# Third unit's query of layer 1 for the third chunk alone, first groups inside the attention; the latents' input projections of layer 0 half a unit later

## The reference, cut to what matters

```
q = (t @ w_query).reshape(nt, 8, 2, 128)
s1, s2 = q[:, :, 0] . sub_k1, q[:, :, 1] . sub_k2      # 128 scores each
v1, i1 = top_k(s1, 16); v2, i2 = top_k(s2, 16)
top_s, top_pos = top_k(v1[:, None] + v2[None, :], 16)  # 16 of 256 pairs
expert_idx = i1 * 128 + i2 at top_pos; gates = softmax(top_s)
out = sum_k gates_k * gelu(t . u_tab[expert_k]) * v_tab[expert_k]
```

## Time and profile before

| | us |
|---|---|
| median of 3 runs (2343.33 to 2344.27) | 2344.12 |
| the profiled execution | 2341.56 |
| its span | 2339.8 |
| busy: PE / DVE / ACT / POOL | 1639.4 / 1551.2 / 875.4 / 944.3 |
| moved by DMA | 927.92 MB, mean 397 GB/s |

### The profile page before, as it was taken

The page is one execution under the profiler, slowest core; times in us unless marked ns, Lnnn a source line. Parts: engine busy times, 40 slices in busy tenths (PEclk is TensorE's granted clock), DMA queues, the critical chain, the costliest instruction groups (busy, mean ns, idle before and its releaser), DMA issues.

```text
span 2339.8 us, 27431 instructions
## 1 busy us (share of the span) xinstructions
PE 1639.4 (70%) x9193; PEld 716.9 (31%) x9193; DVE 1551.2 (66%) x3640; ACT 875.4 (37%) x2596; POOL 944.3 (40%) x840
## 2 busy tenths in 40 slices
PE   7998987777876666766555766678787765555556
PEld 3655543323333222323211212225453311111111
DVE  1227767887767677777767676653868877766654
ACT  2223443445443233443333444442523333332323
POOL 1213244545453444444444454430343545444441
PEclk8999998889898878888777987888998877766788
DMA  9999899999999999999999999994699999999996
GB/s 398 384 370 354 343 390 420 421 420 416 420 413 420 420 419 414 415 414 417 413 417 411 421 420 419 417 388 162 266 386 418 419 422 421 421 421 421 422 421 290
DMA packets 140490, 927.92 MB, mean 397 GB/s; under 512 B 17063, under 2 KB 24007, under 8 KB 33342
## 3 DMA queue, kind: packets, MB, share of 16 engines
q0 software_dynamic: 112816, 807.16, 83.8%
q1 hardware_dynamic: 27390, 119.01, 12.8%
q10 hardware_dynamic: 144, 0.01, 0.0%
HBM read 924.97 MB, written 1.15 MB: 396 GB/s over the span
## 4 chain that ended last, share of the span: by engine, by line
DMA 45%; PE 27%; DVE 16%; issue 5%; ACT 5%; POOL 2%; SPq 0%; POOLq 0%; DVEq 0%; ACTq 0%
DMA arena<-in_uv,small 43%; PE bank L1465 13%; DVE arena L2412 8%; PE bank L797 3%; POOL arena L736 2%; PE bank L762 2%; ACT aux L1728 2%; DMA arena<-in_ada 1%; PE bank L153 1%; PE bank L783 1%; DVE aux L2334 1%; PE bank L944 1%; ACT small L1721 1%; PE bank L1278 1%; PE bank L774 1%
## 5 line engine op out<-in xcount | busy, mean ns | idle before, releaser
L736 POOL DMA_INDIRECT arena<-in_uv,small x765 | 898.9, 1175 | 1173.1 <-PE bank L1465 887.5
L1465 PE MATMUL bank<-arena,aux 64*64 64x512 f32 x5896 | 917.8, 768 | 620.7 <-ACT aux L1728 583.6
L2412 DVE CUSTOM_DVE_ANT_0 arena<-arena,h 128x1024 f32<-128x1024 f32 x765 | 922.8, 1228 | 460.5 <-DMA arena<-in_uv,small 454.2
L1465 PEld LDWEIGHTS bank<-arena,aux 64*64 64x64 f32 x5896 | 259.3, 171 | 1214.2 <-ACT aux L1728 695.7
L1721 ACT ACTIVATE small<-small 128x4 f32<-128x4 f32 (+3 forms) x212 | 43.4, 205 | 1097.0 <-DVE small L2412 1096.9
L1728 ACT ACTIVATE aux<-aux,small 128x64 f32<-128x64 f32 x768 | 206.4, 337 | 7.0 <-ACT small L1721 0.2
L1703 ACT ACTIVATE aux<-small 128x64 f32<-128x64 f32 x768 | 204.4, 336 | 11.6 <-DVEq L2403 2.6
L797 PE MATMUL bank<-hT,aux 128*128 128x256 f32 (+1 forms) x752 | 159.6, 367 | 4.7 <-ACT hT L1534 2.5
L797 PEld LDWEIGHTS bank<-hT,aux 128*128 128x128 f32 x752 | 130.2, 190 | 47.8 <-issue 27.0
L1675 ACT ACT_TABLE_LOAD x73 | 93.7, 1283 | 1.3
L2412 DVE DVE_READ_ACCUMULATOR2_ANT small<- 128x1 f32 x768 | 62.9, 82 | 0.0
(11 more groups left out here) (318 smaller groups left out, 1647.1 us busy)
## 6 DMA issues: line engine op xcount, KB each, us to landing
arena<-in_ada SPq DMA_DIRECT2D x36, 1024.0 KB, 10.3
aux<-in_w_query SPq DMA_DIRECT2D x43, 512.0 KB, 8.2
arena<-in_uv,small POOLq DMA_INDIRECT x765, 15.0
arena<-in_w_head SPq DMA_DIRECT2D x16, 512.0 KB, 10.1
hT<-in_ada SPq DMA_DIRECT2D x7, 1024.0 KB, 8.5
arena<-in_w_qkv SPq DMA_DIRECT2D x3, 2048.0 KB, 14.9
h<-in_ada SPq DMA_DIRECT2D x5, 1024.0 KB, 12.6
arena<-in_w_o SPq DMA_DIRECT2D x4, 1024.0 KB, 10.0
```

Of the source, the lines that this page charges most:

```text
L736: nc.gpsimd.indirect_dma_start(out=slot_at(pos), out_offset=None, in_=d["uv"][unit // FIRST], in_offset=bass.IndirectOffsetOnAxis(ap=self. ...
L1465: last = nc.tensor.matmul(bank[2 * r + m][out:out + 64, :], self.dg[rr, (s + o) % 8, :], slot_at(at)[rr, cols], start=first, stop=False)
L2412: last = nc.vector.tensor_tensor_reduce(out=slot_at(at)[:, 0:D], in0=slot_at(at)[:, 0:D], in1=h[:, c * D:(c + 1) * D], scale=1.0, scalar=0 ...
```

## The change

In layer 0 the input projections of the latents and the steps after them move four positions later, half a unit, up to the first head of the attention, whose last steps are squeezed into the old places:

```diff
 # PE, lat()
-                    yield 5
+                    yield 9
                     pe.wait_ge(nt_copied, 24)
                     in_half(2, 0, bank[6])
-                    yield 7
+                    yield 11
                     in_half(2, 1, bank[7])
 ...
-                    yield 10
+                    yield 15
                     in_half(3, 0, bank[6])
-                    yield 11
+                    yield 16
                     in_half(3, 1, bank[7])
 ...
-                    yield 21      # q_of(0), k_of(0)
+                    yield 25
-                    yield 29      # transposes_of(0)
+                    yield 30
 # ACT, lat()
-                    for c, at in ((2, 7), (3, 13)):
+                    for c, at in ((2, 11), (3, 17)):
 # DVE, lat()
-                    for c, at in ((2, 8), (3, 14)):      # an_mean, an_rope
+                    for c, at in ((2, 12), (3, 18)):
-                    yield 23
+                    yield 25
                     rotate_lat(0)
 # the ring: places 7 to 9 from slot 42, 11 until slot 37
-            early = [*range(7 if n < 34 else 10)]
-            return early + [11] * (n < 30) + [IN_ROWS] * (n >= 16)
+            early = [*range(7 if n < 42 else 10)]
+            return early + [11] * (n < 38) + [IN_ROWS] * (n >= 16)
```

In layer 1 the query of unit 34 is split. Chunk 2's half is made in `second_layer`, in bank 6, with its own copy, score and choice; chunk 3's half stays in `third_job`. Three groups of unit 32 instead of two lie inside the attention, and the first group of unit 33 comes before chunk 3's residual:

```diff
 # ring of layer 1
-        start = (9, 6, 0, 1, 10, 11, 7, 8) * 2 + (9, 6, 0, 1, 2, 3, 4, 5, 12, 13, 14)
+        start = (9, 6, 0, 1, 10, 11, 7, 8) * 3 + (2, 3, 4, 5, 12, 13, 14)
 # PE
+                def third_query():
+                    for side in range(2):
+                        pe.wait_ge(w_q_loaded[side], 32 + 48 * side)
+                        last = queries(self.wq_third[side], side, CTX, P, 0, bank[6])
+                    last.then_inc(q_done, 1)
+                def third_score():
+                    pe.wait_ge(o_copied, last_count(2 * H, 2 * H - 1))
+                    pe.wait_ge(third_stage, 1)
+                    score(0, self.keys_third).then_inc(third_stage, 1)
-                    g_attention(H, {0: next_score, 2: lambda: turned_transposes(7), 4: first_group, 5: tops_taken, 7: second_group})
-                    late_out(0, 3, 5)
-                    combine(FIRST, 2)
-                    late_out(0, 5, H)
-                    late_out(1)
-                    combine(FIRST, 3)
+                    g_attention(H, {0: next_score, 2: lambda: turned_transposes(7), 3: lambda: g_values(H + 1), 4: first_group,
+                                    5: lambda: combine(FIRST, 1), 7: lambda: combine(FIRST, 2), 8: lambda: late_out(0, 0, 3)})
+                    third_query()
+                    late_out(0, 3, 5)
+                    combine(FIRST, 3)
+                    third_score()
+                    late_out(0, 5, H)
+                    late_out(1)
+                    combine(FIRST + 1, 0)
 # ACT
-                    g_attention(H, {2: lambda: turned_copies(7), 3: first_group, 5: lambda: gates(FIRST + 1, False), 6: lambda: group(FIRST, 1)})
-                    group(FIRST, 2)
+                    g_attention(H, {2: first_group, 4: lambda: group(FIRST, 1), 6: third_group})
                     group(FIRST, 3)
+                    third_query_copy()
+                    gated_identities(FIRST + 1, 0)
+                    group(FIRST + 1, 0)
 # DVE
-                    g_attention(H, {0: lambda: raw_scale(7), 1: half_turned, 2: next_tops, 3: lambda: dots(FIRST, 0, range(GRP)),
-                                    4: lambda: choose(FIRST + 1, 1), 5: lambda: dots(FIRST, 1, (0, 1)), 6: lambda: dots(FIRST, 1, (2, 3))},
-                                {4: rest_chosen})
-                    dots(FIRST, 2, range(GRP))
+                    g_attention(H, {0: lambda: raw_scale(7), 1: half_turned, 2: lambda: dots(FIRST, 0, range(GRP)), 3: next_tops,
+                                    4: lambda: dots(FIRST, 1, range(GRP)), 5: lambda: choose(FIRST + 1, 1),
+                                    6: lambda: dots(FIRST, 2, range(GRP))},
+                                {5: rest_chosen})
                     dots(FIRST, 3, range(GRP))
                     finish_gates(FIRST + 1)
+                    dve.wait_ge(third_stage, 2)
+                    for side in range(2):
+                        tops_now(FIRST + 2, side, 0)
+                    dve.sem_inc(tops_done, 1)
+                    for stage in (1, 2, 3):
+                        choose(FIRST + 2, stage)
+                    dots(FIRST + 1, 0, range(GRP))
                     add_half(3, 0, bank[LATE_S[0]], self.ffn_rows1[0], gy_done, 2 * GKV + 1)
```

More of the change, by code:

```diff
@@ L402, in start_of, with ahead @@
             return n % FIRST == 0
+        def ahead(n, g):
+            return n == 0 and g < 2 or (n, g) == (FIRST + 1, 0)
         def idx_count(unit, half=1):
@@ L792, in k_proj, with queries @@
                     last.then_inc(kp_done, 1)
-                def queries(weights, side, lo, width, at):
+                def queries(weights, side, lo, width, at, b=Q_BANK):
                     for k in range(KD):
-                        last = nc.tensor.matmul(Q_BANK[:, side * 256 + at:side * 256 + at + width], weights[:, k, :], hT_at(k, lo, width),
+                        last = nc.tensor.matmul(b[:, side * 256 + at:side * 256 + at + width], weights[:, k, :], hT_at(k, lo, width),
                                                 start=(k == 0), stop=(k == KD - 1))
@@ L828, in third_job @@
                     for side in range(2):
-                        pe.wait_ge(w_q_loaded[side], 32 + 48 * side)
-                        queries(self.wq_third[side], side, CTX, 256, 0).then_inc(q_done, 1)
+                        last = queries(self.wq_third[side], side, CTX + P, P, P)
+                    last.then_inc(q_done, 1)
                 def third_scores():
                     pe.wait_ge(q_copied, 21)
-                    pe.wait_ge(tops_done, 18)
-                    score(0, self.keys_third)
+                    pe.wait_ge(tops_done, 19)
                     score(1, self.keys_third).then_inc(sc_done, 1)
@@ L1320, in g_attention @@
                             g_transposes(first + u - 1)
-                        if 2 <= u < H + 2:
+                        if 2 <= u < H + 2 and u != 3:
                             g_values(first + u - 2)
@@ L1482, in _ @@
                     for g in range(NG):
-                        if n or g > 1:
+                        if not ahead(n, g):
                             combine(n, g)
@@ L1648, in _, with third_query_copy @@
                 scored = S_BANK[:].rearrange("p (s c n) -> p s c n", s=2, c=2)
+                def third_query_copy():
+                    act.wait_ge(q_done, 35)
+                    act.wait_ge(sc_done, 18)
+                    nc.scalar.copy(self.qT[:, :, 0:P], bank[6][:].rearrange("p (s n) -> p s n", s=2)[:, :, 0:P]).then_inc(third_stage, 1)
                 def third_queries():
@@ L1783, in lat @@
                                 nc.scalar.copy(dst, src).then_inc(at_copied, 1)
-                    for c, at in ((2, 18), (3, 20)):
+                    for c, at in ((2, 22), (3, 24)):
                         yield at
@@ L2049, in g_attention @@
                             g_copies(first + u - 1)
-                        if u >= 2:
+                        if u >= 2 and u != 3:
                             g_out_copies(first + u - 2)
@@ L2771, in _ @@
                         elif n == FIRST + 1:
-                            if g == 1:
-                                dve.wait_ge(later_copied, 3)
-                                for side in range(2):
-                                    tops_now(n + 1, side, 0)
-                                dve.sem_inc(tops_done, 1)
-                                for stage in (1, 2, 3):
-                                    choose(n + 1, stage)
                             if g == 3:
```

40 lines of the change are left out of this document (20 added, 20 removed).

## The result

| | before | changed |
|---|---|---|
| median of 12 runs each, us | 2343.56 (2340.28 to 2345.09) | 2349.20 (2345.65 to 2355.61) |
| profiled execution / its span, us | 2341.56 / 2339.8 | 2345.77 / 2344.0 |
| first gather of layer 1, us | 1646.33 | 1642.37 |
| from there to the end of the span, us | 693.5 | 701.6 |

The ratio is 1.0027, interval [1.002, 1.0035]: slower, by 5.6 us between the medians, where 8 us faster were forecast. The last row tells where: layer 1 takes 8.1 us longer, and the 4.0 us by which it starts earlier cover half of that in this execution. In the changed kernel `combine` has line 1479, the gathers 739, the queries 800, the scores 808, `late_out` 1343, the ends of the norm 2231, the tops 2358.

What follows compares the result with a forecast made beforehand. The bound was taken to be one stream of 768 gathers of 1 MB, losing time only where its queue runs dry. Profiled 2341.6 - 8 (layer 0) + 0 (change of layers) = 2333.6; as median 2344.1 - 8 = 2336 us, range 2327 to 2346.

Steps and rivals of the forecast that it cites:

- part 2: Change of layers: 1.7 us gained at the gathers, 1.7 lost behind them; 0 in all, ends -6 and +6.
- part 1: Layer 0: chunk 2's `in_half` matmuls leave unit 0 and unit 1's first group; 8 us saved (3 to 11).
- what stands behind in part 2: Units 33 and 34 shift by 8 us behind the late third chunk; 1 to 3 us may go, 1.7 in the sum.
- the step that removes the hole: Layer 0 entry: `an_mean(2)` no longer stops DVE at 254.5, first gather issued at 259.4, not 272.1; the 5 us gap goes.
- slot 33's gather is issued at 289.3: Layer 0, unit 1: 2.3 us too late for the queue, landing at 294.7, not 304.6; stream 9.9 us ahead.
- 2 us for both, with 0 and 7 as ends: Layer 0: amount given back by the nine-place ring at slot 40 and DVE's wait for `rotate_lat(0)` at position 25.
- = 13.6 us: Change of layers, 1671 to slot 31: gathers 16, 20, 24, 28, 30 late by 1.8, 5.9, 2.2, 2.8, 0.9; before 15.3.
- they take it, the last by a hair: Units 33 and 34: slacks of 12.4 us at gather 39 and 8.3 at gather 55 absorb a shift of 8 us.
- the late third chunk decides: Rival, 0.12: unit 35's query chain 20 us late instead of 8, beyond 8.3 us of slack; 4 us slower, 2348.
- The rule weighed against a third group inside the attention: ACT, change of layers: skill page counts 2.66 us per table switch, 5.3 for the new pair; the row gave 2.6.

Runs made afterwards that it cites:

- e6: Kernel before with the second half of the third chunk's output projection computed twice, 7 us more on TensorE; 2349.34 us, ratio 1.0032.
- e3: Layer 1 part with only unit 32's three groups inside the attention and the new ring order, no split query, layer 0 as before; 2348.68 us, ratio 1.0036.
- e17: e3 with the third group of unit 32 taken out of the attention again; 2341.14 us, ratio 1.0007.
- e19: Changed kernel with the third group of unit 32 taken out of the attention again; 2343.73 us, ratio 1.0005.
- e7: Kernel before with the split query alone, groups, ring and latents unchanged; 2348.34 us, ratio 1.0027.
- e9: e7 with the late queries and score moved ahead of unit 33's second group on TensorE and ScalarE; 2339.55 us, ratio 0.9992.
- e18: e9 plus the change's layer 0 part, two groups of unit 32 inside the attention and the new ring; 2340.41 us, ratio 0.9996.
- e12: Kernel before with only the late queries and scores moved ahead of unit 33's second group on TensorE and ScalarE; 2339.34 us, ratio 0.9997.

## Why the prediction was wrong

Between 8 us faster and 5.6 us slower lie 13.6 us. 6.1 of them are the sum of the late gathers in part 2, 5.3 are part 1, 1.7 are what stands behind in part 2; 0.5 have no place.

**Part 1, the step that removes the hole: right.** No DVE wait before `an_mean` until 284 us, 420 GB/s from 260 to 280.

**Part 1, "slot 33's gather is issued at 289.3": 4.0 us off, and too much kept.** It was issued at 293.31. The wait of DVE was 8.06 us, as said; but PE, idle for 5.03 us, then started `combine(1, 2)` 1.5 us later than said and needed 6.5 us for it, not 3.66. Of what is given back, "2 us for both, with 0 and 7 as ends": the stream was 5.0 us ahead from 310 to 380 and 1.0 at 440, so about 4 went, in unit 3. The 4.0 us by which layer 1 starts earlier are not all gain either. Over twelve profiled executions with the old layer 0 the first gather of layer 1 lies between 1642.97 and 1648.70, mean 1646.5; over eight with the new one between 1642.37 and 1646.41, mean 1643.7. The part is worth about 2.7 us, not 8.

**Part 2, the sum "= 13.6 us" of the late gathers: the step that failed.** It was to be 1.7 us less than before and was 4.4 more: 19.1 against 14.7 in the stretches. The order of the chain and what each gather waits for were right, and gathers 8 and 12 did come earlier; the terms on PE were too small. In old times (3.96 us added) gathers 8, 12, 16, 20 and 24 were issued at 1668.7, 1679.8, 1694.4, 1710.9 and 1722.6, against 1667.1, 1676.9, 1690.5, 1706.4 and 1718.6 as forecast, and the norm was done at 1735.6 against 1731.3. Two terms come to these 4 us by their rows, though no run takes them apart. The combines of groups 1 and 2 stop PE and then take 5.36 us, priced at 3.66: 2 x 1.70 = 3.4 us, and `combine(32, 3)` and `late_out(1)` started 3.6 and 3.4 us later than said. And the forecast let the first gather go 1.9 us after the start of a `combine`; it went 2.8 us after it at groups 0 and 3. The other 2 of the 6.1 us stay open. Both terms stood in the trace of the kernel before, where the gathers after these rows were issued at 1673.66 and 1688.54:

```profile
1669.28 5.36 PE L1465 MATMUL bank<-arena,aux 64*64 64x512 f32 x32 [2.46 <-ACT aux L1728]
...
1685.75 3.66 PE L1465 MATMUL bank<-arena,aux 64*64 64x512 f32 x32
```

That this lateness costs in full is what e6 shows: 6.9 us lost for 6.9 us of delay, nearly all by gather 30, because gathers 20 to 31 wait in turn for `late_out(1)`, the norm and the third query with the queue dry. And without the third group inside most of the loss goes: 7.5 us of layer 1 from e3 to e17, 5.1 from the changed kernel to e19.

**Part 2, "they take it, the last by a hair": did not hold, for the same reason.** The forecast had unit 35 8 us late and 12.4 and 8.3 us of slack at gathers 39 and 55. Unit 35 was 11.6 us late. That is 3.3 us beyond the 8.3, and 3.4 us were lost, where the sum had 1.7. They were lost at gather 51, though, whose slack had not been read, so that the agreement may be luck.

**The rival that came nearest** was "the late third chunk decides" (chance 0.12, 2348 us). Its place was right: `combine(33, 2)` behind unit 35's query (e7 against e9). Its condition, a delay of 20 us that decides only from 16, was not: 11.6 us did, and most of the loss stood ahead of that `combine`. That its 2348 us lies near the measured 2349.2 is luck. Slower had a chance of 0.13 in all, too small for a sum whose two parts rested on the same price of a `combine`.

**The rule weighed against a third group inside the attention** was ScalarE's table load, 1.28 us by the row. It was not the cost: the load was over before the dots were (1682.85 above), and what cost was PE's wait for the diagonals.

## What to carry to other kernels

In an in-order list, a step put "beside" a chain costs the chain its wait as well as its work: 3.66 us of products took 9.6 us of PE's list here. Price such a step by the row of one that has waited, not by the row of one that has not. A slack measured at one transfer holds for that transfer; before using it, look at every other one that the same chain releases, or delay the chain by a known amount and time it. When a list of indices comes earlier, see whose turn it took: e7's eleven early microseconds stood ahead of the group behind which the next query waited.

## What the runs showed of the hardware

TensorE's clock decides the price of a waiting `combine`. Stretches of the changed kernel: the wait before `combine(32, 1)` and the `combine` itself, then the first part of `combine(1, 2)` in layer 0; the figure before the DMA share is the granted clock.

```profile
1668.70:1672.40 3.70, 0.00 (x0) 0.00 (x0) 3.66 (x9) 1.81 (x5) 2.20 (x2) 1.00 0.99 368
1672.40:1677.80 5.40, 5.35 (x33) 1.64 (x33) 4.99 (x18) 3.60 (x10) 1.65 (x2) 0.68 1.05 413
```
```profile
288.70:292.20 3.50, 3.42 (x16) 1.04 (x20) 3.18 (x9) 3.42 (x10) 0.00 (x0) 0.50 0.54 220
```

After 3.8 us without a matmul the same 32 matmuls ran at a mean clock of 0.68 of full speed in 5.36 us, part of the time at the lower of the two levels, 1.2 GHz; after 5.03 us of idling the first 3.5 us lay wholly at it. The length of one wait does not settle it: after 1.46 us without a matmul `combine(33, 1)` took 3.66 us in e9 (1739.56 above, clock 1.00) and 5.36 us in e18, clock 0.68 from 1735.0 to 1740.3. By the Trainium skill, TensorE: Matmul & The Clock Gate (Part 1, the HAM clock gate), "the default state is throttled, and activity releases the throttle"; the trace agrees in these stretches.

Nothing in the change touches layer 0's entry in e12, yet its first gather of layer 1 came 3.4 us earlier than in the kernel before: a single profiled execution places a stage no better than that, and a stage is better compared by the time inside it.
